# Rows of tokens gathered for two expert pairs at a time, combine in four banks, and loads in the order in which places come free

## What is computed

```python
scores = sigmoid(h @ w_router)            # 16 experts in 4 groups
# top group, then its top 2 experts; gates = their scores, made to sum to 1
out = 0
for e in range(16):
    y = (silu(h @ w_gate[e]) * (h @ w_up[e])) @ w_down[e]   # 1024 -> 512 -> 1024
    out = out + gates[:, e:e+1] * y
h = layer_norm(alpha * h + out)
```

## Time and profile before

| | |
|---|---|
| runs | 651.45, 651.89, 651.88 us, median 651.88 |
| span of the profiled execution, first to last instruction | 650.5 us |
| mean granted TensorE clock | 0.995 |
| experts of layer 0 on PE | 112.8 to 322.8 us |
| experts of layer 1 on PE | 429.5 to 640.0 us |
| DMA | 240.79 MB, mean 370 GB/s |

### The profile page before, as it was taken

How to read it: one execution, slowest core, us unless ns; L and a number is a source line. 1 busy time by engine, 2 the same in 40 slices (tenths; PEclk the granted TensorE clock), 3 DMA queues, 4 the chain that set the end, 5 groups by cost and what they waited for, 6 DMA issues and landing times.

```text
span 650.5 us, 7970 instructions
## 1 busy us (share of the span) xinstructions
PE 635.9 (98%) x3227; PEld 344.4 (53%) x3227; DVE 311.2 (48%) x600; ACT 195.1 (30%) x389; POOL 134.6 (21%) x125
## 2 busy tenths in 40 slices
PE   8999999999999999999999999999999999999993
PEld 5887886453333443333488878764433344333431
DVE  6598997622033020320678989893032040320326
ACT  5832963240010221110193377351210032110111
POOL 1899300700000000000049960042000000000000
PEclk9999999999999999999999999999999999999998
DMA  8991299899999999999996118999999999999991
GB/s 360 433 391 66 102 430 428 358 434 422 430 426 426 432 425 427 427 427 429 427 426 297 50 66 316 430 368 418 429 431 424 430 426 425 430 424 431 427 391 67
DMA packets 18330, 240.79 MB, mean 370 GB/s; under 512 B 2032, under 2 KB 2160, under 8 KB 3440
## 3 DMA queue, kind: packets, MB, share of 16 engines
q1 hardware_dynamic: 17136, 234.46, 85.4%
q10 hardware_dynamic: 1152, 5.77, 2.2%
HBM read 239.17 MB, written 1.05 MB: 369 GB/s over the span
## 4 chain that ended last, share of the span: by engine, by line
PE 87%; DMA 5%; DVE 5%; issue 1%; ACT 1%; DVEq 0%
PE bank L694 31%; PE bank L715 16%; PE bank L586 13%; PE bank L743 5%; PE bank L560 5%; DMA ring<-in_units 5%; PE bank L667 2%; PE bank L805 2%; PE bank L817 2%; PE bank L647 2%; DVE w_split L1395 1%; PE bank L627 1%; PE bank L574 1%; PE bank L704 1%; PE bank L887 1%
## 5 line engine op out<-in xcount | busy, mean ns | idle before, releaser
L694 PE MATMUL bank<-ring,xe 128*64 128x512 f32 x1024 | 223.6, 593 | 0.6 <-DMA ring<-in_units 0.6
L694 PEld LDWEIGHTS bank<-ring,xe 128*64 128x64 f32 x1024 | 74.5, 137 | 143.1 <-issue 139.8
L715 PE MATMUL bank<-ring,area_b 128*64 128x512 f32 x512 | 113.8, 596 | 0.2
L1598 DVE TENSOR_TENSOR area_b<-area_b,bank 128x512 f32<-128x512 f32 x16 | 11.0, 688 | 209.4 <-PE bank L694 209.4
L1215 POOL TENSOR_TENSOR rstd<-var_eps,half_neg 128x1 f32<-128x1 f32 x18 | 10.6, 592 | 467.3 <-DVE var_eps L1327 467.3
L1248 POOL TENSOR_TENSOR in_lo<-ring,in_hi 128x512 fp32r<-128x512 f32 x56 | 71.2, 1328 | 13.6 <-ACT in_hi L1015 13.6
L715 PEld LDWEIGHTS bank<-ring,area_b 128*64 128x64 f32 x512 | 35.2, 137 | 66.7 <-issue 64.9
L1618 DVE SCALAR_TENSOR_TENSOR y_lo<-bank,slot_gate,y_hi 128x512 fp32r<-128x512 f32 x32 | 24.0, 751 | 85.0 <-ACT y_hi L1108 85.0
L1094 ACT ACTIVATE area_b<-bank 128x512 f32<-128x512 f32 x16 | 9.6, 597 | 163.8 <-PE bank L694 163.8
L1108 ACT ACTIVATE y_hi<-bank,slot_gate 128x512 fp32r<-128x512 f32 x32 | 22.0, 687 | 96.3 <-PE bank L715 96.3
L1675 DVE SCALAR_TENSOR_TENSOR bank<-mix,small,bank 128x256 f32<-128x256 f32 x116 | 45.6, 484 | 0.0
(11 more groups left out here) (204 smaller groups left out, 797.0 us busy)
## 6 DMA issues: line engine op xcount, KB each, us to landing
ring<-in_units SPq DMA_DIRECT2D x109, 2048.0 KB, 23.2
ln_par<-in_ln_rows ACTq DMA_DIRECT2D x4, 1024.0 KB, 8.4
ring<-in_units SPq DMA_DIRECT2D x2, 1024.0 KB, 8.2
h<-in_x SPq DMA_DIRECT2D x2, 512.0 KB, 4.2
piece_area<-in_branch_rows ACTq DMA_DIRECT2D x2, 512.0 KB, 5.5
ln_par<-in_ln_rows SPq DMA_DIRECT2D x1, 1024.0 KB, 36.1
piece_area<-in_sgw_cols ACTq DMA_DIRECT2D x2, 256.0 KB, 5.8
out<-h SPq DMA_DIRECT2D x1, 512.0 KB, 2.7
```

Of the source, the lines that this page charges most:

```text
L694: mm = pe.matmul(bank[2 + m][e * SLOTS:(e + 1) * SLOTS, :], xe[:, k, at + e * SLOTS:at + (e + 1) * SLOTS], w[:, c, m, e, :], start=k == 0, ...
L715: mm = pe.matmul(bank[5 + n][e * SLOTS:(e + 1) * SLOTS, :], hidT[:, k, e * SLOTS:(e + 1) * SLOTS], w[:, k, e, :], start=k == 0, stop=k == ...
```

## The change

- `GROUP` is 2: `xe` and `pick` hold two pairs. The first two pairs are gathered together before pair 0 (`first_pairs`, 32 matmuls of 256 columns). `other_pairs` is gone. The rows of the next two pairs are gathered while the odd pairs 1, 3 and 5 are computed: two chunks (eight matmuls of 256 columns) after each of units 0, 1 and 2 of gate and up, and two at the start of the second half of down.
- Combine has four banks: 7, 4, 3 and 0 or 1 by the pair's parity. The waits for DVE's adds move to the next use of each bank.
- The transposes of the weighted picks come ahead of those of `hid`. DVE copies `hidT` before the four adds, and makes the next group's `pick` in even pairs.
- The experts' units are loaded in the order 0, 3, 4, 5, 1, 2, 6, ...: units 3, 4 and 5 wait for slabs 1, 2 and 3 to be used, units 1 and 2 for five used units. Unit 9 of each layer doesn't go into the ring but into `extra`, 16 KB per partition over `area_a` and a part of `area_b`, once the output projection's chunks are used. A layer then takes 54 turns of the ring, six rounds of nine.
- Small tiles move to other places of `area_b`; `hid` is written over `silu`. The "more" rounds get a ring of six.

The core of the diff:

```diff
-GROUP = 4
+EXTRA = RING
+RING_UNITS = LAYER_UNITS - 1
+LOAD_ORDER = (0, 3, 4, 5, 1, 2) + tuple(range(6, PAIR_UNITS * PAIRS))
+GROUP = 2
-COMB_BANKS, LAST_COMB_BANKS = (7, 4, 7, 4), (7, 4, 2, 3)
+NEXT_BANKS, MORE_BANKS = (0, 7, 4, 7), (0, 1, 7, 4)
+COMB_BANKS, LAST_COMB_BANKS = ((7, 4, 3, 0), (7, 4, 3, 1)), (7, 4, 2, 3)
...
+            def load_experts(l):
+                for k in LOAD_ORDER:
+                    src = units[l, SLABS + k]
+                    if k == EXTRA:
+                        sp.wait_ge(chunk_used, 2 * KC * (l + 1))
+                        sp.dma_start(extra[:, :], src).then_inc(extra_landed, 16)
+                        continue
+                    n = ring_unit(l, k)
+                    if k in (1, 2):
+                        sp.wait_ge(used, l * LAYER_UNITS + 5)
+                    elif n >= RING:
+                        sp.wait_ge(used, used_by(n - RING))
+                    sp.dma_start(unit_at(n), src).then_inc(landed[n % RING], 16)
...
+                def gather(g, p):
+                    dst = bank[(NEXT_BANKS if ps.main else MORE_BANKS)[p]]
+                    for c in (2 * p, 2 * p + 1):
+                        half = slice(c % 2 * GROUP * P, (c % 2 + 1) * GROUP * P)
                         for b in range(TB):
+                            wait_pick(g, b)
                             for part in (n_hi, n_lo):
+                                mm = pe.matmul(dst[:, half], part[:, b, c * P:(c + 1) * P], pick[:, b, :],
+                                               start=c % 2 == 0 and b == 0 and part is n_hi, stop=b == TB - 1 and part is n_lo,
+                                               skip_group_check=True)
+                    mm.then_inc(s["gathered"], 1)
...
                 def turn_pick(j):
                     nth("pick_w", j)
+                    if j >= 2:
+                        added(j - 2, 4)
...
                 def gate_up(j):
...
                         mm.then_inc(ps.used, 1)
+                        if gathers_next(j) and u < CHUNK_PAIRS - 1:
+                            if u == 0:
+                                nth("back", j - 1)
+                            elif j >= 2:
+                                added(j - 2, u)
+                            gather(g + 1, u)
...
                 def down(j):
...
+                            if gathers_next(j) and n == 1 and k == 0:
+                                added(j - 1, 1)
+                                gather(j // GROUP + 1, CHUNK_PAIRS - 1)
...
                 def combine(j, parts):
...
-                        if banks[k] == COMB_BANKS[k] and k >= 2:
-                            added(j, k - 1)
-                        elif k < 2 and j:
-                            added(j - 1, k + 3)
+                        if k < 2 and j:
+                            added(j - 1, k + 1)
+                        if k < 2 and j + 1 < pairs and gathers_next(j + 1):
+                            wait_xe(j // GROUP + 1, 4 + 2 * k)
...
                     gate_up(j)
+                    if j:
                         combine(j - 1, (0, 1))
-                        turn_hid(j)
+                    turn_pick(j)
+                    turn_hid(j)
+                    if j:
                         combine(j - 1, (2, 3))
-                        turn_pick(j)
                     down(j)
-                    if j == 0 and ps.main:
-                        other_pairs(range(2, KC))
-                    if (j + 1) % GROUP == 0 and j + 1 < pairs:
-                        gather((j + 1) // GROUP, range(0, 4))
```

More of the change, by code:

```diff
@@ L261, in trunk @@
                                           [area_b_at + 8192, uv_at + 8192, uv_at + 12288])]
-        scratch_at = [ring_at + 4 * UNIT * ((l * LAYER_UNITS + RING - 1) % RING) for l in range(DEPTH)]
+        scratch_at = [ring_at + 4 * UNIT * ((l * RING_UNITS + RING - 1) % RING) for l in range(DEPTH)]
         xi_hi = [nc.alloc_sbuf_tensor_at(f"xi_hi{l}", [P, KC, SEQ], F32R, offset=scratch_at[l]) for l in range(DEPTH)]
@@ L388, in __init__ @@
                 self.landed = landed_sems
-                self.chunks, self.picks = GATHERS[name]
+                self.gathers, self.picked = GATHERS[name]
         def moe_sems(name):
@@ L398, in trunk @@
         for l in range(DEPTH):
[L399 removed]
+            m = Pass("main", used, landed, l * RING_UNITS + SLABS, l * LAYER_UNITS + SLABS, l * PAIRS, 1)
             m.s = main_sems
@@ L451, in load_slab, with load_more @@
                     sp.dma_start(unit_at(n), src).then_inc(landed[n % RING], 16)
[L453 to L469, removed]
+            def load_experts(l):
[9 more added lines that the diff above has]
+                    elif n >= RING:
+                        sp.wait_ge(used, used_by(n - RING))
+                    sp.dma_start(unit_at(n), src).then_inc(landed[n % RING], 16)
+            def load_more(l, ps, rnd, it):
+                for k in range(GROUP * PAIR_UNITS):
+                    turn = rnd * (ITERS * GROUP * PAIR_UNITS) + it * (GROUP * PAIR_UNITS)
+                    sp.wait_ge(ps.used, turn + (k + 1))
+                    at = k % MORE_RING
+                    src = units[l, bass.ds(it * (GROUP * PAIR_UNITS) + (SLABS + k), 1)].rearrange("o p n -> p (o n)")
+                    sp.dma_start(ring[:, at, :], src).then_inc(ps.landed[at], 16)
             for l in range(DEPTH):
@@ L601, in nth, with before @@
                     pe.wait_ge(s[name], pairs_before * per + ((ps.pair0 + j) * per + k))
-                def before(g, per, parts):
-                    return groups_before * per + (l * per + (g + 1) * parts if ps.main else g * parts)
+                def before(per):
+                    return (l if ps.main else groups_before) * per
                 def wait_pick(g, b):
-                    pe.wait_ge(s["pick"], before(g, ps.picks, TB) + (b + 1))
+                    pe.wait_ge(s["pick"], before(ps.picked * TB) + (g * TB + b + 1))
@@ L611, in wait_xe @@
                 def wait_xe(g, k):
-                    pe.wait_ge(s["xe"], before(g, ps.chunks, KC) + k)
+                    pe.wait_ge(s["xe"], before(ps.gathers * KC) + (g * KC + k))
                 def landed_unit(k):
-                    at = (ps.unit0 + k) % ps.ring
+                    if ps.main and k == EXTRA:
+                        pe.wait_ge(extra_landed, 16 * (l + 1))
+                        return extra[:, :]
+                    n = ring_unit(l, k) if ps.main else k
+                    at = n % ps.ring
@@ L617, in landed_unit, with first_pairs @@
                     turns = rnd * (ITERS * TURNS * 16) + it * (TURNS * 16)
-                    pe.wait_ge(ps.landed[at], turns + 16 * ((ps.load0 + k) // ps.ring + 1))
+                    pe.wait_ge(ps.landed[at], turns + 16 * (n // ps.ring + 1))
                     return ring[:, at, :]
-                def first_pair(part):
+                def first_pairs(part):
                     for b in range(TB):
-                        pe.wait_ge(s["pick"], l * ps.picks + (b + 1))
+                        wait_pick(0, b)
@@ L629, in first_pair @@
+                            mm = pe.matmul(bank[FIRST_BANKS[c // 2]][:, half], part[:, b, c * P:(c + 1) * P], pick[:, b, :],
+                                           start=b == 0 and part is n_hi and c % 2 == 0, stop=b == TB - 1 and part is n_lo,
                                            skip_group_check=True)
-                            if b == TB - 1 and part is n_lo:
+                            if b == TB - 1 and part is n_lo and c % 2 == 1:
                                 mm.then_inc(s["gathered"], 1)
[L633 to L642, removed]
+                def gather(g, p):
+                    dst = bank[(NEXT_BANKS if ps.main else MORE_BANKS)[p]]
+                    for c in (2 * p, 2 * p + 1):
+                        half = slice(c % 2 * GROUP * P, (c % 2 + 1) * GROUP * P)
@@ L672, in turn_pick, with gathers_next @@
+                    mm.then_inc(s["gathered"], 1)
+                def gathers_next(j):
+                    return ps.main and j % GROUP == GROUP - 1 and j + 1 < pairs
                 def turn_pick(j):
                     nth("pick_w", j)
+                    if j >= 2:
+                        added(j - 2, 4)
                     for b in range(TB):
@@ L686, in gate_up @@
                             k = 2 * u + c
[L687 to L690, removed]
-                            elif j % GROUP == 0 and m == 0:
-                                wait_xe(g, max(k + 1, 2) if ps.main else k + 1)
+                            if j % GROUP == 0 and m == 0:
+                                wait_xe(g, k + 1)
+                            if j >= 2 and k == 0 and m == 1:
+                                added(j - 2, 3)
                             for e in range(2):
@@ L748, in experts @@
                 if ps.main:
-                    first_pair(n_hi)
-                    first_pair(n_lo)
-                else:
```

(27 more changed lines are left out.)

143 lines of the change are left out of this document (56 added, 87 removed).

## The result

The change makes the kernel slower by a little: 653.34 us median (653.11 to 653.50, 10 runs) against 651.84 us (651.45 to 652.58, 10 runs), a ratio of 1.0022 with a 95% interval of 1.0013 to 1.0031. Forecast were 656.6 us and slower. The sign is right and the time lies in the range, but the move is 1.5 us where 4.7 were forecast. The gather blocks cost what was forecast; the step that failed is combine, whose part was put at 0.1 us a pair and is 0.27, as the experiments show.

What follows compares the result with a forecast made beforehand. PE's own work was taken to bound the kernel: per layer -12.55 + 16.0 + 0.1 - 0.7 = +2.85 us, two layers +5.7, less 1.0 of DMA waits, +4.7, giving 656.6 us; range 652.3 to 659.8.

Steps and rivals of the forecast that it cites:

- The gather blocks: Twelve new blocks a layer, between gate and up units and inside down: 1.33 us each, 16.0 us per layer added.
- PE is the bound, the change adds to its work: Whole kernel: PE busy 635.9 of 650.5 us, 87% of the chain; added gathers outweigh the removed ones.
- The blocks before: Old gathers in the experts' pairs: taking them out was to save 12.55 us per layer.
- Combine, "It hardly did": Combine's second half hardly waited for DVE; four banks and transposes together save 0.1 us in seven pairs, -0.7 a layer.
- First gather: Gather before pair 0: 32 matmuls of 256 instead of 128 columns, 3.84 us against 3.76, +0.1 per layer.
- Sum: Per layer -12.55 + 16.0 + 0.1 - 0.7 = +2.85; two layers +5.7, less 1.0 of waits: +4.7 us.
- the 1.4: Time around the profiled span: 650.5 us span against 651.88 median, 1.4 us taken as unchanged.
- Loads: Experts' units land one transfer, about 4.9 us, sooner; PE's 1.0 us of waits at the layers' ends goes.
- the hidden or shorter switch: At gather blocks: fixed price of 0.37 us vanishes (647.7, chance 0.07) or only 0.2 is paid (652.5, chance 0.13).
- rival 4: Experts' units: loads do not come earlier, a place still waited for in order; 1.0 us stays, 657.6, chance 0.06.
- rival 3: Inside gather blocks: four waits for the picks each cost some 0.02 us, 2 us more, 658.6; chance 0.15.
- rival 2: At gather blocks: the switch is shorter for narrow matmuls, only entry paid, 0.2 us a block, 652.5; chance 0.13.

Runs made afterwards that it cites:

- four banks: The kernel before with only combine in four banks and the adds' waits moved; gathers, loads and transposes as before: 651.80 us, ratio 0.9996.
- order: The kernel before with only the transposes of the weighted picks moved ahead of those of the product: 651.58 us, ratio 0.9995.
- one block: The changed kernel with each group's 32 gather matmuls in one block instead of four: 647.16 us; with the loads of the kernel before as well, 652.04 us.

## Why the prediction was right or wrong

- **PE is the bound, the change adds to its work**: right. The blocks cost 1.30 us, forecast 1.33; twelve a layer are 15.6 us for 16.0. The blocks before cost what was taken: 12.55 us a layer by the rows, 12.6 if pair 1 is measured whole.
- **Combine, "It hardly did"**: wrong, and this is the step that failed. The text looked at the fourth part's wait (0.24 us at the weight load) and took it for the matmuls' pace. That wait is worth some 0.07 us. The larger one, 0.22, lay one part earlier, ahead of combine's second half, where the profile names no engine ("issue"). The term is 0.27 us a pair, not 0.1 (nor the upper end, 0.2): 14 x 0.17 = 2.4 us of the 3.2 us that the forecast was off. Undoing this part alone costs 3.8 us.
- **First gather**: 4.04 us against 3.76, +0.3 a layer, where 0.1 was taken. Blocks and first gather together: -0.8 and +0.4.
- **Sum**: per layer -12.6 + 15.6 + 0.3 - 1.9 = +1.4, two layers +2.8, less 1.0 of waits: +1.8. The spans differ by 1.3 and the medians by 1.5. By the chain the experts of layer 0 take 1.10 us more and those of layer 1, which had the longer wait, 0.55. Against that, DVE's last row of `stats` and its next pass over `h` at the very end lie 0.65 us apart and not 0.91; why was not followed. In every run that lists both, time and span are 1.7 to 1.9 us apart, not 1.4: the profiled execution of the kernel before took about 652.3 us, 0.4 above its median, which is where 1.3 and 1.5 part. In the forecast the 1.4 cancels.
- **Loads**: right for this kernel, in part by luck. The 1.0 us of waits is gone, but the changed kernel loses it with the old loads too. The text read the small waits as DMA having room. The runs show the opposite: the kernel before ran level with its loads, and a faster PE could gain nothing. Three edits that make PE faster (four banks, order, one block) each end between 651.6 and 652.1 without the own place.
- **Rivals**: the hidden or shorter switch is out, and so are loads that don't come earlier (rival 4). The price of 0.34 to 0.36 us comes out of three numbers of blocks, and for blocks of 256 columns it is what it was for 512 (0.37). So the Trainium skill's pull-ahead of weight loads (TensorE: Matmul & The Clock Gate, Part 3, The mechanism) did not cover these switches; PEld idles 19.5 us in all ahead of the 24 blocks of the changed kernel, 0.8 each (idle time of the weight load, of which PE loses 0.35). The waits for the picks (rival 3) cost nothing: inside a block the matmuls follow at 0.12 us with them, the pace of the row without them.

PEld's group and two rows inside a block of the changed kernel (groups with shapes apart; PE's timeline):

```profile
L667 PEld LDWEIGHTS bank<-pick,n_hi 128*128 128x128 f32 x96 | 18.2, 189 | 19.5 <-issue 19.5
```

```profile
143.77 0.28 PE L667 MATMUL bank<-pick,n_lo 128*128 128x256 f32 x1
143.89 0.28 PE L667 MATMUL bank<-pick,n_hi 128*128 128x256 f32 x1
```

## What to carry to other kernels

A small wait for DMA at the end of a long stretch can mean that two engines run level: a faster PE then gained nothing until the transfers had one more place, and its test alone showed nothing. (The new loads alone were tried in the changed kernel only, not in the kernel before.) Count the switches between kinds of matmul as well as the matmuls: here each block put into the stream of weights cost about 0.35 us, with 8, 16 or 32 matmuls in it. Where a wait may be hidden under "issue", compare the distance between two instructions with the same distance where no wait is possible.

## What was not expected of the hardware

Not every change of kind on PE has a price. PE's timeline of the changed kernel, where combine follows transposes:

```profile
288.10 0.60 PE L712 MATMUL bank<-small,area_b 128*128 128x128 f32 x4
...
288.45 0.48 PE L754 MATMUL bank<-y_hi,back 128*128 128x512 f32 x1
288.77 0.40 PE L754 MATMUL bank<-y_lo,back 128*128 128x512 f32 x1
```

and where a gather block follows the experts' half-array matmuls:

```profile
143.02 0.60 PE L696 MATMUL bank<-ring,xe 128*64 128x512 f32 x2
143.55 0.38 PE L667 MATMUL bank<-pick,n_hi 128*128 128x256 f32 x1
```

Combine begins 0.35 us after the first of four transposes, no more than their own time; the gather begins 0.53 us after the last two expert matmuls, where 0.43 is their step. Its second matmul follows after 0.22 us (143.77) where 0.12 is the pace, and the unit behind takes 0.15 more. Together 0.10 + 0.10 + 0.15 = 0.35: the fixed price, most of it on the way in, as rival 2 had it, but with a way back that is paid too. Two remedies of one wait gave 0.28 and 0.21 us a pair alone and 0.27 together.
